# Start addresses of some split operands in SBUF moved by 64 or 128 bytes

## The reference, cut to what matters

```
def hier_moe(h, ...):                  # per group g, experts e of width 256
    hid = silu(h @ w_gate[g]) * (h @ w_up[g])
    out = out + einsum("blef,ble,efd->bld", hid, comb[:, :, g], w_down[g])

def swiglu(h, w13, w2):                # four layers, hidden width 2816
    g, u = split(h @ w13, 2)
    return (silu(g) * u) @ w2

merged = sigmoid(g_ssd) * y_ssd + sigmoid(g_att) * y_att
return merged @ w_out
```

## The kernel before, in words

| product | stationary | moving | |
|---|---|---|---|
| L974 | ring, 0 | h or g, 64 | differs |
| L993, L1379 | h or g, 64 | ring, 0 | differs |
| L1308, L1321 | hid, 64 | ring, 0 | differs |
| L1538 visits 0, 1 | h, 64 | ring, 0 | differs |
| L1538 visit 3 | own, 64 | ring, 0 | differs |
| L1538 visits 2, 4 | own, 64 | second, 64 | agrees |
| L1502 after visits 0, 1, 3 | hid, 64 | ring, 0 | differs |
| L1502 after visits 2, 4 | hid, 64 | second, 64 | agrees |

## Time and profile before

### The profile page before, as it was taken

How to read it: one execution, slowest core, us unless ns; L and a number is a source line. 1 busy time by engine, 2 the same in 40 slices (tenths; PEclk the granted TensorE clock), 3 DMA queues, 4 the chain that set the end, 5 groups by cost and what they waited for, 6 DMA issues and landing times.

```text
span 1959.4 us, 32460 instructions
## 1 busy us (share of the span) xinstructions
PE 1894.4 (97%) x13360; PEld 1728.1 (88%) x13360; DVE 1374.6 (70%) x1578; ACT 921.2 (47%) x991; POOL 46.2 (2%) x67
## 2 busy tenths in 40 slices
PE   6999998899999999999999999999989999999999
PEld 6998888788888889999999999987879999999998
DVE  5777977776777766666668666678997566676665
ACT  5544745555666663433345443335334333444332
POOL 0000000000000000001101000000000000000000
PEclk8999999999999999999999999999999999999999
DMA  7553343687788747555553285552324555555553
GB/s 222 175 170 99 128 144 144 257 308 279 270 305 302 280 142 209 194 193 193 193 173 127 92 274 193 193 193 70 103 86 151 193 193 193 172 194 172 193 193 107
DMA packets 243787, 365.97 MB, mean 187 GB/s; under 512 B 12558, under 2 KB 217833, under 8 KB 231273
## 3 DMA queue, kind: packets, MB, share of 16 engines
q1 hardware_dynamic: 243689, 364.58, 55.2%
HBM read 363.51 MB, written 1.05 MB: 186 GB/s over the span
## 4 chain that ended last, share of the span: by engine, by line
PE 82%; DVE 11%; ACT 2%; issue 2%; DMA 2%; SPq 1%; POOL 0%; DVEq 0%; ACTq 0%; POOLq 0%
PE proj L974 37%; PE acc L1308 11%; PE proj L1538 11%; PE proj L993 7%; PE acc L1502 6%; DVE ring_lo L2569 3%; DMA raw<-in_a_w_in_dram 1%; PE acc L1321 1%; PE proj L1842 1%; PE acc L1018 1%; ACT ring_hi L1993 1%; PE proj L1681 1%; PE acc L1774 1%; PE misc L1481 0%; PE acc L1639 0%
## 5 line engine op out<-in xcount | busy, mean ns | idle before, releaser
L2569 DVE TENSOR_TENSOR ring_lo<-raw,ring_hi 128x2048 fp32r<-128x2048 f32 x242 | 560.2, 2317 | 223.1 <-ACT ring_hi L1993 221.9
L1993 ACT ACTIVATE ring_hi<-raw 128x2048 fp32r<-128x2048 f32 x242 | 462.3, 1914 | 440.8 <-PE proj L974 185.6
L974 PE MATMUL proj<-h_hi,ring_hi 128*128 128x256 f32 x1424 | 407.9, 286 | 7.7 <-DVE ring_lo L2569 7.6
L974 PE MATMUL proj<-h_lo,ring_hi 128*128 128x256 f32 x1424 | 396.3, 278 | 0.0
L974 PE MATMUL proj<-h_hi,ring_lo 128*128 128x256 f32 x1424 | 396.2, 278 | 0.0
L974 PE MATMUL proj<-g_hi,ring_hi 128*128 128x256 f32 x1088 | 303.2, 279 | 2.1 <-DVE ring_lo L2569 2.1
L974 PE MATMUL proj<-g_lo,ring_hi 128*128 128x256 f32 x1088 | 301.5, 277 | 0.0
L974 PE MATMUL proj<-g_hi,ring_lo 128*128 128x256 f32 x1088 | 301.4, 277 | 0.0
L974 PEld LDWEIGHTS proj<-h_hi,ring_hi 128*128 128x128 f32 x1424 | 269.1, 189 | 19.8 <-issue 9.8
L974 PEld LDWEIGHTS proj<-h_lo,ring_hi 128*128 128x128 f32 x1424 | 269.7, 189 | 4.0 <-issue 3.1
L974 PEld LDWEIGHTS proj<-h_hi,ring_lo 128*128 128x128 f32 x1424 | 268.9, 189 | 0.0
(11 more groups left out here) (461 smaller groups left out, 3439.3 us busy)
## 6 DMA issues: line engine op xcount, KB each, us to landing
raw<-in_f_w_dram SPq DMA_DIRECT2D x132, 1024.0 KB, 5.0
raw<-in_w_in_dram SPq DMA_DIRECT2D x29, 1024.0 KB, 5.4
raw<-in_w_exp_gate_dram SPq DMA_DIRECT2D x25, 1024.0 KB, 5.7
raw<-in_w_exp_up_dram SPq DMA_DIRECT2D x24, 1024.0 KB, 4.8
raw<-in_a_w_in_dram SPq DMA_DIRECT2D x24, 1024.0 KB, 5.1
raw<-in_w_exp_down_dram SPq DMA_DIRECT2D x23, 1024.0 KB, 6.0
raw<-in_b_w_qkv_dram SPq DMA_DIRECT2D x12, 1024.0 KB, 5.1
raw<-in_c_w_in_dram SPq DMA_DIRECT2D x12, 1024.0 KB, 5.1
```

Of the source, the lines that this page charges most:

```text
L974: last = pe.matmul(bank[:, a, :], w[:, k, a * P:(a + 1) * P], h[:, k, :], start=(k == 0 and w is hi and h is h_h and (a == 0 or not first) ...
L1993: act.activation(w_hi[n.slot][:, :], raw[n.slot][:, :], ACT.Copy).then_inc(hi_ready, 1)
L2569: dve.tensor_tensor(w_lo[n.slot][:, :], raw[n.slot][:, :], w_hi[n.slot][:, :].bitcast(f32), SUB)\
```

## The change

`own_*`, `second_*`, `hid_*` and `ple_y` are moved 64 bytes up (with `hid_*` also 1 KB down), so that they start on multiples of 128. `silu_e` and `hid` move out of their way by whole KB. `merged` gets tiles of its own, 128 bytes above `g_hi` and `g_lo`. No instruction, wait or semaphore is added or removed.

```
+        merged_hi = at("merged_hi", [P, KT, SEQ], 78 * KB + 128, f32r)
+        merged_lo = at("merged_lo", [P, KT, SEQ], 92 * KB + 128, f32r)
-        own_hi = [at(f"own_hi{q}", [P, KT, P], (8 + 4 * q) * KB, f32r) for q in range(N_GROUPS - 1)]
-        own_lo = [at(f"own_lo{q}", [P, KT, P], (20 + 4 * q) * KB, f32r) for q in range(N_GROUPS - 1)]
+        own_hi = [at(f"own_hi{q}", [P, KT, P], (8 + 4 * q) * KB + 64, f32r) for q in range(N_GROUPS - 1)]
+        own_lo = [at(f"own_lo{q}", [P, KT, P], (20 + 4 * q) * KB + 64, f32r) for q in range(N_GROUPS - 1)]
-        ple_y = at("ple_y", [P, TT * D], 32 * KB)
+        ple_y = at("ple_y", [P, TT * D], 32 * KB + 64)
-        sets_hi = [ring_hi, at("second_hi", [P, RING, CHUNK], 60 * KB, f32r)]
-        sets_lo = [ring_lo, at("second_lo", [P, RING, CHUNK], 84 * KB, f32r)]
+        sets_hi = [ring_hi, at("second_hi", [P, RING, CHUNK], 60 * KB + 64, f32r)]
+        sets_lo = [ring_lo, at("second_lo", [P, RING, CHUNK], 84 * KB + 64, f32r)]
-        silu_e = at("silu_e", [P, COLS], 40 * KB)
+        silu_e = at("silu_e", [P, COLS], 41 * KB)
-        hid = at("hid", [P, 2, SEQ], 42 * KB)
+        hid = at("hid", [P, 2, SEQ], 104 * KB)
-        hid_hi = at("hid_hi", [P, 2, SEQ], 44 * KB, f32r)
-        hid_lo = at("hid_lo", [P, 2, SEQ], 46 * KB, f32r)
+        hid_hi = at("hid_hi", [P, 2, SEQ], 43 * KB + 64, f32r)
+        hid_lo = at("hid_lo", [P, 2, SEQ], 45 * KB + 64, f32r)
...
+            if operand == "merged":
+                return merged_hi, merged_lo
...
-                            for h, w in ((g_hi, hi), (g_hi, lo), (g_lo, hi)):
+                            for h, w in ((merged_hi, hi), (merged_hi, lo), (merged_lo, hi)):
...
-                link(dve.tensor_copy(g_hi[:, tiles, :], pj[:, tiles, :]))
-                dve.tensor_tensor(g_lo[:, tiles, :], pj[:, tiles, :], g_hi[:, tiles, :].bitcast(f32), SUB).then_inc(m_split, 1)
+                link(dve.tensor_copy(merged_hi[:, tiles, :], pj[:, tiles, :]))
+                dve.tensor_tensor(merged_lo[:, tiles, :], pj[:, tiles, :], merged_hi[:, tiles, :].bitcast(f32), SUB).then_inc(m_split, 1)
```

More of the change, by code:

```diff
@@ L661, in parts_of @@
                 return (ssd_hi, ssd_lo) if operand == "ssd" else (attn_hi, attn_lo)
-            return (g_hi, g_lo) if operand in ("merged", "mix0", "ffn0", "na", "hyena", "mix3", "ffn3") else (h_hi, h_lo)
+            if operand == "merged":
+                return merged_hi, merged_lo
+            return (g_hi, g_lo) if operand in ("mix0", "ffn0", "na", "hyena", "mix3", "ffn3") else (h_hi, h_lo)
         def gain_of(operand, k):
@@ L1377, in terms @@
                         for t in range(TT):
-                            for h, w in ((g_hi, hi), (g_hi, lo), (g_lo, hi)):
+                            for h, w in ((merged_hi, hi), (merged_hi, lo), (merged_lo, hi)):
                                 last = pe.matmul(merged_bank(j)[:, t, :], h[:, k, t * P:(t + 1) * P], w[:, k, :],
-                                                 start=(k == 0 and t == 0 and w is hi and h is g_hi),
-                                                 stop=(k == KT - 1 and h is g_lo), skip_group_check=True)
+                                                 start=(k == 0 and t == 0 and w is hi and h is merged_hi),
+                                                 stop=(k == KT - 1 and h is merged_lo), skip_group_check=True)
                     return last
```

## The result

The change made the kernel slower: 1973.05 us in the median against 1964.68 us for the kernel before on the same chip, six executions of each, ratio 1.0044 with a 95% interval of 1.0034 to 1.0054. The prediction was 1962.0 us, with a range of 1957.5 to 1969.0: the kernel was to get faster and got slower. The profiled execution took 1972.35 us (span 1970.6), 11.2 us more than the one of before.

A forecast was written before the change was run, and what follows sets the result against it. TensorE, busy 97% of the span, was taken as the bound. Savings of 1.2 (experts), 1.2 (down products in rounds), 0.3 and 0.1 us (first and last ones) gave 1964.8 - 2.8 = 1962.0 us, range 1957.5 to 1969.0.

The forecast's parts named there:

- L974 behind the down product: Feed-forward rounds: the 256-column matmuls after an agreeing down product stay fast, 0 taken; other end 15.7 us lost.
- the rounds lock into the slow pace: Rival: an agreeing down product leaves L974 at 117.8 ns all round, 15.7 us more, 1979.3 us; chance 0.18.
- Down products: Feed-forward rounds: the pair comes to agree and saves 0 to 81 ns a round; 30 taken, 1.2 us over 40.
- First downs: Each feed-forward layer's first down product, at 233.3 ns, falls to 226.5 at best, 0.65 us; 0.3 us taken.
- Experts: Expert loop: more blocks settle and fewer entries cost time, 150 ns less a turn, 1.2 us over 8 turns.
- unsettled: Expert loop: five agreeing blocks of 12 matmuls not yet at their fastest, 4.3 ns each, 258 ns before and after.
- Only the moving operand counts: Rival on 512 columns: the moving operand's remainder alone decides; rounds stay, experts save 1.1 us, 1963.7 us; chance 0.15.
- Addresses do nothing: Rival: levels come from the order of instructions and where they stand, the change is void, 1964.8 us; chance 0.09.
- ScalarE and VectorE nothing: Writing the moved tiles 64 bytes higher costs these engines 0; bounds 0.1 us either way, hidden behind PE.
- merged nothing: Moving merged by 128 bytes leaves its pair differing; 0 taken, a turn of pace worth 0.42 us either way.
- 16.8 means the slow pace: Sign in a feed-forward round: 16.32 to 16.40 us was expected, 16.8 would show the slow pace.
- agrees or differs: TensorE matmuls: whether both operands' starts share a remainder after 128 sets the level, 226.5 settled or 228.75 ns on 512 columns.

The follow-up runs named there:

- e1: Kernel before with hid_* alone moved (silu_e and hid out of their way): 1976.4 us, ratio 1.0077.
- e3: Changed kernel with two transposes added behind spread_inv in every feed-forward layer: 1969.4 us, ratio 1.0030 against the kernel before.
- e2: Changed kernel with hid_* back at 44 and 46 KB, the rest still moved: 1963.2 us, ratio 1.0003 against the kernel before.
- e5: Changed kernel whose gated layers use hid tiles of their own at the old place; experts keep the new one: 1960.5 us, ratio 0.9992 against before.
- e7: Changed kernel with hid_lo alone back at 46 KB: 1964.5 us, ratio 1.0010 against the kernel before.
- e4: Kernel before with an unused 64-byte tile ahead of h_hi, moving all activations against the rings: 1993.8 us, ratio 1.0166.
- e11: Changed kernel with merged_* back at 78 and 92 KB, without the 128 bytes: 1973.6 us, ratio 1.0047 against the kernel before.
- e10: Kernel before with an unused 128-byte tile ahead of h_hi, moving all activations against the rings: 1987.1 us, ratio 1.0111.
- f1: Changed kernel with hid_* 128 bytes higher still, at 43 and 45 KB + 192: 1967.0 us, ratio 1.0026 against the kernel before.
- f2: Kernel before with the 64-byte neg_half allocated ahead of the rings, which move 64 bytes up alone: 1995.5 us, ratio 1.0172.
- e6: Changed kernel with old-place hid tiles for the gated layers and two transposes behind spread_inv in each feed-forward layer: 1957.1 us, ratio 0.9976 against before.
- e9: Kernel before, addresses untouched, with two transposes behind spread_inv in the four feed-forward layers: 1962.1 us, ratio 0.9988.
- e12: Kernel of e6 with the two transposes also behind spread_inv of the first and last mixer: 1957.7 us, ratio 0.9966 against the kernel before.
- e8: Changed kernel with two transposes behind every down product of the feed-forward loop: 1975.9 us, ratio 1.0068 against the kernel before.

## Why the prediction was wrong

- **The failed step is the term for L974 behind the down product: "I take that it does, as both kinds of exit seen so far do: 0".** The text gave this exit as the one that no row shows, with 15.7 us behind it, and then took the two exits that rows 6 and 7 do show as a sample of it. Both belong to pairs that differ. The agreeing exit leaves the slow pace (e1, e3), in all rounds but the one above: 96 x 4.45 = 0.43 us lost in each, where the prediction had 0. With hid back in the gated layers it is gone (e2, e5), and with a third of the matmuls back too (e7).
- **The rival "the rounds lock into the slow pace" is what happened.** Its 1979.3 us was too high. It let the down products save nothing and counted eight of the 96 out; measured is 0.35 us a round, 11.8 over the 36 distances. And the experts gave more than the 1.2 us it set against the loss.
- **Down products.** The term was 0.03 us a round, "nearer to the slow settling". They settle at once: 226.7 throughout, the 54 ns of the optimistic end; the 27 ns of entry went too. First downs, costed at 0.3: from 839.75 to 845.22 us it is 5.47 / 24 = 227.9 ns in after, 4 x 24 x 5.4 = 0.52 us saved. PE's timeline of after:
```profile
839.75 0.63 PE L1312 MATMUL acc<-ring_hi,hid_hi 128*128 128x512 f32 x2
...
845.22 0.28 PE L978 MATMUL proj<-g_hi,ring_hi 128*128 128x256 f32 x1
```
- **Experts.** 0.15 us a turn was predicted, 0.26 measured (1.79 in seven turns). (The matmuls from 423.33 in the earlier trace rows are the first half of visit 4, as the prediction counts them.) The five "unsettled" dozens, 258 ns, were not a cost of agreeing pairs in general: ten to twelve slow matmuls in before, three to six in after. Why the same agreement settles sooner at the new place stays open: in e4 own and second set stand at 128 as in after, and the block behind the transposes there takes ten again.
- **Only the moving operand counts** (0.15): refuted. In after the ring stays and hid moves, and the level goes from 228.75 to 226.7. **Addresses do nothing** (0.09): refuted by e1. The page of the Trainium skill named there, "SBUF — State Buffer", Specifications (TRN2), with lines of 16 bytes as the only unit, does not account for these levels: all starts here are whole lines, and 64 bytes are worth up to 5.8% on 256 columns (113.3 to 119.9).
- **ScalarE and VectorE nothing, merged nothing**: right (2289 against 2290; e11).
- The signs named for the slow pace held: "16.8 means the slow pace" is the 16.75 in the window.

The reading "agrees or differs", by the remainder after 128, was too coarse. With d the start of the stationary minus that of the moving operand, modulo 256, as the program allocates them (ring 128; before: h, g, own, hid, second 64; after: own, hid, second 128, h and g 64), the levels once settled are (512 columns: the rounds, and for e1 the experts):

| d | 512 columns, ns | 256 columns, ns |
|---|---|---|
| 0 | 226.7 (after) | 119.9 (e4) |
| +64 | 233.3 (e10; e1, second set) | 113.3 or 117.8 (before, after) |
| 128 | 232.1 to 232.5 (f1, f2) | 118.6 or 120.0 (f2) |
| -64 | 228.75 (before) | 113.3 or 117.8 (e10, L975) |

In e10 the down product stands at +64 and L975 at -64. Its rounds are slow, but not because -64 has no fast pace: outside the feed-forward layers L975 of e10 has 90 matmuls in 10.20 us, 113.3 ns.
```profile
792.16 0.28 PE L975 MATMUL proj<-g_hi,ring_hi 128*128 128x256 f32 x1
...
802.36 0.28 PE L975 MATMUL proj<-g_hi,ring_hi 128*128 128x256 f32 x1
```
What is shown: on 512 columns the distance decides the level (e1, e4, e10, f1, f2, each with one group moved; 0, +64 and 128 each occur at two different pairs of places, with one level). On 256 columns it decides which paces occur; in e4, at distance 0, no chunk came near 113.3. Where there are two paces, the exit of one product decides which the next one keeps (e1, e3, e7, f1): a down product at distance 0 leaves the slow one, at -64 or 128 the fast one. Behind the one of e10, at +64, the rounds are slow; whether it makes the slow pace or only hands it on was not tried. Not shown is why: nothing here sees inside the engine. Nor was a move by 256 of one operand alone tried, which would test the period; and why before's pairs at 64 and 64, also d = 0, settle later than after's at 128 and 128 is open, as is what makes the last mixer fall fast or slow from one kernel to the next.

## What to carry to other kernels

Where one engine is busy without a gap, read start-to-start distances by product, and note which levels occur and what stands ahead of each. When a change alters a product, the product behind it can lose more than the changed one wins: bound that exit at its bad end and try the smallest edit that shows it before moving many tiles. Where two operands can be placed freely, choose their distance per product, here 0 for 512 columns in the experts, -64 for the down products that have 256-column products behind them, and +64 for these. As e5 has it so and is not clear of the kernel before (0.9992 [0.9979, 1.0005]), the gain from this is small here; it is the wrong choice that costs.

## What had not been expected of the hardware

- TensorE keeps one of two paces on 256 columns, 113.3 and 117.8 ns, for hundreds of matmuls with nothing changed (528 in 59.86 or in 62.19 us). In f2 the two are 118.6 and 120.0.
- Two 128-column transposes behind `spread_inv` bring the fast pace (e3, e6, e9, e12: 144 matmuls in 16.35 instead of 16.96 us), and behind the down products of a loop the rounds are fast and slow in turn (e8). Why one brings the fast pace and the other does not is open.
- The placement of the rings against everything else is worth 1.7% of the kernel (f2, 1995.5 us) with no instruction changed.
